# Modulation rows in four column tiles of TensorE's array, in a hybrid diffusion backbone

## The reference, cut to what matters

```python
def adaln_params(cond, w, b):
    """cond (N, D) -> six (N, 1, D) tensors: shift/scale/gate for mixer and channel mixer."""
    mod = (jax.nn.silu(cond) @ w + b)[:, None, :]
    return jnp.split(mod, 6, axis=-1)

sh1, sc1, g1, sh2, sc2, g2 = adaln_params(c, ada_w[i], ada_b[i])          # latent
csh1, csc1, cg1, csh2, csc2, cg2 = adaln_params(c_ctx[None, :], ada_w[i], ada_b[i])  # context
a = rms_norm(h, norm_g[i, 0]) * (1.0 + sc1) + sh1
```

## Time and profile before

| | |
|---|---|
| median of 3 runs | 3206.22 us |
| profiled execution | 3205.24 us |
| its span | 3203.4 us |
| PE matmul busy | 2918.4 us, 91% |
| DVE busy | 2087.8 us, 65% |
| ACT busy | 1277.2 us, 40% |
| line 1537, 640 records of the slots | 152.9 us |
| mean DMA rate | 82 GB/s |

### The profile page before, as it was taken

The page is one execution under the profiler, slowest core; times in us unless marked ns, Lnnn a source line. Parts: engine busy times, 40 slices in busy tenths (PEclk is TensorE's granted clock), DMA queues, the critical chain, the costliest instruction groups (busy, mean ns, idle before and its releaser), DMA issues.

```text
span 3203.4 us, 44914 instructions
## 1 busy us (share of the span) xinstructions
PE 2918.4 (91%) x17196; PEld 2522.1 (79%) x17196; DVE 2087.8 (65%) x2939; ACT 1277.2 (40%) x1847; POOL 124.8 (4%) x176
## 2 busy tenths in 40 slices
PE   7999989999999899999986789899758999999996
PEld 4777767999999899999965567676548899878785
DVE  3789988888965675566554466566266465684665
ACT  3222144433445353334423356566324334443332
POOL 0000000000000000000000012232000000000000
PEclk8999999999999999999988889999878999999998
DMA  6343432222222222222221110000112323333332
GB/s 245 119 145 132 145 112 92 68 92 93 86 79 66 73 60 91 92 78 87 79 71 59 49 32 1 1 1 1 57 55 62 96 88 97 98 92 118 98 95 76
DMA packets 66480, 263.03 MB, mean 82 GB/s; under 512 B 6928, under 2 KB 7184, under 8 KB 60048
## 3 DMA queue, kind: packets, MB, share of 16 engines
q1 hardware_dynamic: 57280, 211.07, 20.9%
q0 software_dynamic: 5760, 41.95, 3.6%
q10 hardware_dynamic: 3280, 7.78, 0.7%
HBM read 256.58 MB, written 4.19 MB: 81 GB/s over the span
## 4 chain that ended last, share of the span: by engine, by line
PE 77%; DVE 13%; ACT 7%; issue 2%; DMA 1%; POOL 0%; DVEq 0%; SPq 0%; ACTq 0%
PE PS L1509 61%; PE PS L1537 4%; PE PS L1746 4%; PE PS L1733 2%; DVE w_lo L905 1%; PE PS L1719 1%; DVE rms L948 1%; DVE cgv L1279 1%; PE PS L1720 1%; PE PS L1517 1%; DVE cgv L1288 1%; DVE h L1000 1%; ACT a_hi L498 1%; ACT prob L884 1%; PE PS L1544 1%
## 5 line engine op out<-in xcount | busy, mean ns | idle before, releaser
L1509 PE MATMUL PS<-a_hi,w_hi 128*128 128x322 f32 (+6 forms) x3456 | 887.5, 325 | 82.9 <-DVE a_lo L980 51.0
L1509 PE MATMUL PS<-a_lo,w_hi 128*128 128x322 f32 (+6 forms) x3456 | 871.8, 320 | 0.0
L1509 PE MATMUL PS<-a_hi,w_lo 128*128 128x322 f32 (+6 forms) x3456 | 871.3, 320 | 0.0
L1509 PEld LDWEIGHTS PS<-a_hi,w_hi 128*128 128x128 f32 x3456 | 589.6, 191 | 136.9 <-issue 60.2
L1509 PEld LDWEIGHTS PS<-a_lo,w_hi 128*128 128x128 f32 x3456 | 592.6, 191 | 25.2 <-issue 2.1
L1509 PEld LDWEIGHTS PS<-a_hi,w_lo 128*128 128x128 f32 x3456 | 590.2, 191 | 25.4
L905 DVE TENSOR_TENSOR w_lo<-raw,w_hi 128x1024 fp32r<-128x1024 f32 (+2 forms) x380 | 443.7, 1172 | 250.6 <-ACT w_hi L445 244.2
L445 ACT ACTIVATE w_hi<-raw 128x1024 fp32r<-128x1024 f32 (+2 forms) x380 | 386.2, 1017 | 1.6 <-DVE zB L1377 1.4
L1509 PE MATMUL PS<-z_hi,w_hi 128*128 128x320 f32 (+1 forms) x1056 | 300.8, 339 | 30.4 <-DVE z_lo L1264 28.3
L1509 PE MATMUL PS<-z_lo,w_hi 128*128 128x320 f32 (+1 forms) x1056 | 298.5, 337 | 0.0
L1509 PE MATMUL PS<-z_hi,w_lo 128*128 128x320 f32 (+1 forms) x1056 | 298.4, 337 | 0.0
(11 more groups left out here) (226 smaller groups left out, 3436.7 us busy)
## 6 DMA issues: line engine op xcount, KB each, us to landing
raw<-wstream SPq DMA_DIRECT2D x380, 512.0 KB, 3.5
ada_slot<-adastream POOLq DMA_DIRECT2D x40, 1024.0 KB, 5.2
ada_first<-adastream SPq DMA_DIRECT2D x4, 2048.0 KB, 19.8
h<-xT SPq DMA_DIRECT2D x1, 2640.0 KB, 14.6
h<-xT ACTq DMA_DIRECT2D x1, 2480.0 KB, 10.8
out<-h ACTq DMA_DIRECT2D x1, 2048.0 KB, 9.3
out<-h ACTq DMA_DIRECT2D x2, 1024.0 KB, 4.3
rope_sb<-rope ACTq DMA_DIRECT2D x1, 1024.0 KB, 4.8
```

The source lines that it names most:

```text
L1509: last = MM(PS[:, 2 * j + m, 0:n], wt[:, j, k, :], mv[:, k, m * n:(m + 1) * n], start=(k == 0 and p_ == 0), stop=(k == tiles - 1 and p_ == 2))
```

## The change

The stationary operand `silu_c` gets 32 columns, of which the first two hold silu(c) and silu(c_ctx) and the others zero. Block k of a group goes to column tile k mod 4 of the array, so to partitions 32*(k mod 4) and on of PSUM. Each tile sums two blocks, k and k + 4. ACT copies all 128 partitions. The turn contracts over 128 partitions with `pick`, a 128 x 2 matrix with ones at rows 32j and 32j + 1, which adds the four parts. `silu_c` moves to a place beside `ada_row`, and POOL sets it to zero at the start.

```diff
-        ada_row = sb("ada_row", [2, 2, 2 * P], F32, rU + 8 * GA)
+        ada_row = sb("ada_row", [P, 2, 2 * P], F32, rU + 8 * GA)
+        silu_c = sb("silu_c", [P, KT, 32], F32, rU + 8 * GA + 16 * P)
...
-        silu_c = sb("silu_c", [P, KT, 2], F32, take(64))
...
+            nc.gpsimd.memset(silu_c[:], 0.0)
             nc.gpsimd.memset(eps_t[:], EPS).then_inc(eps_set, 1)
...
-                A(ada_row[:, g % 2], PS[0:2, 6 + g % 2, 0:2 * P], ACT.Copy).then_inc(row_ready, 1)
+                A(ada_row[:, g % 2], PS[:, 6 + g % 2, 0:2 * P], ACT.Copy).then_inc(row_ready, 1)
...
-            A(silu_c[:], cond, ACT.Silu).then_inc(cond_ready, 1)
+            A(silu_c[:, :, 0:2], cond, ACT.Silu).then_inc(cond_ready, 1)
...
                 for k in range(KT):
-                    last = MM(PS[0:2, 6 + g % 2, 0:2 * P], silu_c[:, k, :], weights[:, k, :], start=(k == 0), stop=(k == KT - 1))
+                    c0 = 32 * (k % 4)
+                    last = MM(PS[c0:c0 + 32, 6 + g % 2, 0:2 * P], silu_c[:, k, :], weights[:, k, :], start=(k < 4), stop=(k >= 4),
+                              tile_position=(0, c0))
                 last.then_inc(ada_used, 1)
...
                 for r in range(2):
-                    last = MM(ada_sums(2 * g + r, 1), ada_row[:, g % 2, r * P:(r + 1) * P], ident[0:2, 0:2], start=True, stop=True)
+                    last = MM(ada_sums(2 * g + r, 1), ada_row[:, g % 2, r * P:(r + 1) * P], vec_sb[:, ds(VEC["pick"][0], 2)],
+                              start=True, stop=True)
...
-                          np.broadcast_to(x["attn_sink"][0][None, :], (P, NQ)), conv_cols(0), conv_cols(1)], axis=1)
+                          np.broadcast_to(x["attn_sink"][0][None, :], (P, NQ)), conv_cols(0), conv_cols(1),
+                          np.tile(np.eye(32, 2, dtype=np.float32), (4, 1))], axis=1)
```

More of the change, by code:

```diff
@@ L56, in _vec_layout @@
                     ("ln_g", 8), ("ln_b", 8), ("b_out", 8), ("cond", 16), ("sink", 16),
-                    ("cw0", 4 * 2 * FT), ("cw1", 4 * 2 * FT)):
+                    ("cw0", 4 * 2 * FT), ("cw1", 4 * 2 * FT), ("pick", 2)):
         VEC[name] = (at, n)
@@ L208, in backbone @@
         ug, uv, cg, cv = u_both[:, 0], u_both[:, 1], cgv[:, 0], cgv[:, 1]
-        ada_row = sb("ada_row", [2, 2, 2 * P], F32, rU + 8 * GA)
-        assert rU + 8 * GA + 16 * P <= rT
+        ada_row = sb("ada_row", [P, 2, 2 * P], F32, rU + 8 * GA)
+        silu_c = sb("silu_c", [P, KT, 32], F32, rU + 8 * GA + 16 * P)
+        assert rU + 8 * GA + 16 * P + KT * 128 <= rT
         T = sb("T", [P, KT, GA], F32, rT)
```

## The result

The changed kernel takes 3162.36 us (median of 4 runs, 3160.22 to 3165.9), the kernel before 3210.03 us (4 runs, 3206.09 to 3216.38). The ratio is 0.9851, with an interval of 0.9829 to 0.9873: 1.5% faster. The kernel before falls into two clusters in all series (3205 to 3207 and 3213 to 3219 us), so its median moves by up to 8 us with the number of runs in each. I therefore compare mainly the two profiled executions: 3203.4 and 3160.5 us, 42.9 us apart.

A forecast was written before the change was run, and what follows sets the result against it. PE was taken as the bound (77% of the span). Nine rounds per group save PE 73 us, of which seven places sum to 42.7, so 3205.24 becomes 3162.5, about 3163; own range 3156 to 3172, 8 in 10 3147 to 3220.

The forecast's parts named there:

- DVE's cap: GLU stages: DVE's depthwise convolution is close behind PE (20.43 of 23.20 us in a first-stage step) and cuts off PE's gain.
- place 4: Second GLU stage, first four steps: DVE's 20.26 us and a hand-off hold a step at 20.4; gain 6.7 us.
- the two steps after it: Second GLU stage, next two steps: gain nothing, since DVE is busy 47.88 of 48.20 us.
- place 5: LayerNorm end: the average and ACT's silu each wait behind a group, 1.5 us each; gain 3.0 us.
- rival 1: All four column tiles run side by side: 2.5 us less per group, sum 54.3 us, 3151 us; chance 0.20.
- Start: Up to the first mod row: average starts at 27.3, mod at 42.2 instead of 48.63; gain 6.4 us.
- First GLU stage: Five steps fall from 23.2 to 20.6 us, hand-off last; with the stall step and last two, gain 19.4 us.
- Gap and out projection: Gap ahead of the out projection: two groups alone, 6.03 to 4.0 and 3.54 to 2.02 us; gain 3.5 us.
- After the last mod: Rest of the kernel, after 563 us: nothing changes.
- places 4 and 7: Second GLU stage's first four steps, 6.7 us; the join, where groups delaying the root end earlier, 1.9 us.
- places 2 and 5: First slot group, at half clock, 6.19 to 4.0 us with 0.4 given back, gain 1.8; LayerNorm end, 3.0 us.
- hand-off of `w_lo`: First GLU stage: 2.04 us from DVE's product to w_lo ends last; each step's second group gives only some 1.1 us.

The follow-up runs named there:

- filler: Changed kernel plus bf16 matmuls nobody reads, 6 behind the second group of each GLU step and 20 ahead of two root waits; 3159.44 us.
- Two tiles: Changed kernel with a group's eight blocks on two column tiles instead of four, four blocks each; 3169.62 us.
- early split: Changed kernel with DVE's split of the next step's first weights ahead of its GLU product, in seven of eight steps per stage; 3156.84 us.
- filler and early split: Changed kernel with both edits, the unread bf16 matmuls on PE and DVE's weight split ahead of its product; 3156.13 us.
- its repetition: The changed kernel measured and profiled again without any edit; 3161.37 us.
- same tile next: Changed kernel with four tiles in the order 0,0,1,1,2,2,3,3, so neighbouring products share a tile; 3161.09 us.
- product on GpSimd: Changed kernel with early split, and the GLU product moved from DVE to GpSimd between its DMA issues; 3167.26 us.
- product on GpSimd with filler: Changed kernel with early split, the GLU product on GpSimd, and the filler matmuls on PE; 3161.58 us.
- one tile: Changed kernel with all eight blocks on one column tile, still 32 stationary columns; 3207.78 us, ratio 0.9991 to the kernel before.

## Why the prediction came out right, and where it was wrong inside

The time (3163 forecast, 3162.4 measured) and the sum (42.7 us forecast, 42.9 between the profiled executions) agree. The mechanism of the group doesn't.

*Two errors then cancelled, and that is luck.* From start to next start each group gave 1.02 us more than I had counted (1.00 instead of 2.02), 49 us in all. DVE's cap took some of it, as I had worked out: in place 4, the two steps after it and place 5 prediction and rival 1 differ by 1.3 us only. By rival 1's sum 11.6 us should still have come out on top. They went as follows:
- Start, 1.75 us short. PE now idles 6.9 us ahead of the second quarter of the weights, where it was 1.4, and its records up to the average have the length of half clock. A group takes 1.94, a turn 1.02, and the average 2.55 us instead of 1.38. The column of the granted clock does not show it (1.00 from 0 to 44 us), so the half clock is read from the durations here:
```profile
25.44 1.94 PE L1539 MATMUL PS<-ada_first,silu_c 128*32 128x256 f32 x16
28.18 2.55 PE L1518 MATMUL PS<-T,cst 128*128 128x330 f32 x4
...
43.98 0.25 DVE L957 TENSOR_TENSOR mod<-PS,vec_sb 128x16 f32<-128x16 f32 x2
```
  I had put the average at 27.3 and mod at 42.2; they came at 28.18 and 43.98 (by my own terms mod would be at 42.0). Of the 0.9 us at the average, 0.4 are the load, which landed that much later (22.63 instead of 22.22).
- First GLU stage, 2.8 us short of rival 1. Step for step, before 23.1 23.2 29.9 23.2 23.2 23.2 26.3 19.2, after 19.5 20.6 25.3 21.0 21.0 19.6 24.2 18.0. The 20.6 of my forecast does occur, but for another reason: DVE is full in it. Two steps have 21.0 at clock 0.92.
- Gap and out projection, 4.2 us short. From 406 to 420 the clock is 0.50; both groups there take 1.94 us, as against the 2.0 or so that I had for one and the 1.1 of rival 1, and the turns around them take 1.01. Up to the first unit 4.9 us are gained; then the units of the out projection lose 2.6 of them, since they start at half clock (59.8 us at 0.95 instead of 57.2 at 1.00):
```profile
409.53 1.01 PE L1547 MATMUL PS<-vec_sb,ada_row 128*128 128x2 f32 x4 [7.45 <-ACT ada_row L453]
410.47 1.94 PE L1539 MATMUL PS<-ada_slot,silu_c 128*32 128x256 f32 x16
...
417.16 0.89 PE L1510 MATMUL PS<-a_hi,w_hi 128*128 128x322 f32 x2
```
- After the last mod, 1.9 us, and 0.7 and 0.2 in places 4 and 7. With the small differences in places 2 and 5 (-0.2 and 0.1) it is 1.75 + 2.8 + 4.2 + 1.9 + 0.7 + 0.2 - 0.2 + 0.1 = 11.45, within rounding the 54.3 - 42.9 = 11.4 to be explained.

Not foreseen was thus the clock: a faster group leaves PE with gaps, and the work around them is paid at half clock. The filler confirms it for the first GLU stage (clock back to 1.00, 4.2 of its 4.6 us to the last mod). For the start and the gap it stands on these rows alone; no run tested it there. The Trainium skill ("TensorE: Matmul & The Clock Gate", Part 1) describes a clock gate that follows how busy the engine has been. This case's rows agree (0.98 for the region from 60 us to the last mod before the change, 0.90 after). Held against the gaps that I had forecast myself, it would have been a bound of the sum.

*Would the sum have held for a group of the forecast's length?* Two tiles are the test, with 1.85 us from start to next start. They gain 40.7 us to the last mod, 2.0 less than my 42.7 for a group that was even 0.17 us longer, and 37.7 us in the time. So the sum was 2 to 5 us too high for its own group.

*The cap by DVE: right.* The stretch from 364 to 412 kept its 48.2 us, and with half the convolution it fell to 40.7, where in the kernel before it fell to 45.9 and PE then filled it. What I put on the hand-off of `w_lo` in the first stage was half right: PE does wait there (1.68 us), but the early split shortens few steps, as DVE has no room.

*What stays open.* PE's saving is 122 us, and 44.8 arrive at the last mod. Half of the convolution accounts for 19 of the difference, filler and early split for 10.6; no run shows what each of the other causes takes of the rest (the second half of the convolution, the hand-offs, the waits for the roots, the half clock at the start and in the gap).

In some profiled executions the second feed-forward network of layer 0 (1216 to 1416 us), whose instructions are the same in all, takes longer, and with it the way from the last mod to the end (2643.3 instead of 2638 us). Two tiles, the filler and filler with early split had it; the changed kernel, its repetition, same tile next, the early split and both kernels with the product on GpSimd did not. The same hundred microseconds, counted from the last mod, first with the filler, then in the changed kernel (columns as above):

```profile
1216.90:1316.90 100.00, 96.88 (x642) 96.62 (x641) 53.97 (x83) 33.38 (x42) 0.00 (x0) 0.97 0.28 90
```
```profile
1222.40:1322.40 100.00, 96.88 (x660) 96.61 (x660) 57.02 (x87) 33.54 (x43) 0.00 (x0) 1.00 0.29 89
```

PE is equally busy, but at 0.97 it gets through 642 matmuls instead of 660. Why the clock drops there I can't say. The filler is neither needed for it (two tiles have it without) nor enough (product on GpSimd with filler: 2637.9). With the order before, this way varies as well: 2636.2 us in the kernel before, 2643.3 with half of the convolution, 2647.1 with one tile. In the profiled executions it is also why the 4.6 us at the last mod don't show at the end.

## What to carry to other kernels

Here matmuls with few stationary columns went on column tiles at next to no cost, and both passes of an fp32 product overlapped with those of other tiles; two tiles already halved the time. Count the saving per group only where the next engine has room, and cost everything near PE's new gaps at half clock too, as one bound of the sum. Before work is moved to GpSimd, look at how long DVE's own operations take beside it. A total that fits is no proof of its terms: here only the group's span and the ledger by place showed that two wrong terms had cancelled, so write down such a span ahead for each step.

## What was not expected of the hardware

- Four column tiles start their fp32 passes together, and each takes its next pass alone: 3.64, 1.92 and 1.07 us for one, two and four tiles, 1.09 us with the same tile twice in a row.
- Of first-stage steps in which PE was idle for 1.7 to 2.3 us, some had a granted clock of 0.92 and others of 1.00, and which ones they were differed between executions of one kernel. The first step took 19.50 us in the first profile and in the repetition (columns of the stages):
```profile
74.90:95.90 21.00, 19.25 (x140) 18.04 (x136) 18.62 (x25) 8.24 (x8) 1.06 (x2) 0.92 0.42 151
```
  The same 140 matmuls were busy for 17.75 us in the first.
- A product of 659 columns on GpSimd takes 1.58 to 5.25 us beside DVE at work, where DVE takes 0.85 us. Beside such products operations of DVE that take 0.88 us took 1.36 and 1.60 us, without a wait in the trace.
- Half of the convolution left out in the kernel before takes 100 us of DVE's work out of the first 567 us (437.9 busy before, 337.9 then), and changes the time by nothing (ratio 1.0003).
